# Norms, rotation and gates of two mixers beside their projections, keys doubled beside the memory's output, values in 384 and 256 columns

## The reference, cut

```python
qa, ka, va, oa, ga, qb, kb, vb = split(h @ w_in)          # 4x512, 16 gates, 512, 128, 128
qb, kb = rms_norm(qb, q_norm_g), rms_norm(kb, k_norm_g)    # per head of 64
ha = mlstm_bidir(qa, ka * 128**-0.5, va, gates)            # 4 heads of 128, both directions
qb_l, kb_l = apply_rope(qb_l, cos, sin), apply_rope(kb_l, cos, sin)   # latent tokens only
ob = banded_window_attention(qb, kb, vb, sink)             # 8 heads, 2 key heads, blocks of 128, window 128
y = concatenate([rms_norm(ha) * sigmoid(oa), ob]) @ w_out
# c_mixer: 8 heads of 128, 2 key heads; norm and rotation of q and k, full attention over 768 keys
```

## Time and profile before

| | us |
|---|---|
| median of 3 runs | 4294.96 |
| profiled execution | 4294.03 |
| its span, first to last instruction | 4292.0 |
| TensorE / VectorE / ScalarE busy | 3920.2 / 2089.8 / 1296.7 |
| first projection, gates, memory with output (from 50.6) | 204.4, 19.3, 131.6 |
| norm, rotation, doubling; first attention | 40.2, 170.6 |
| second projection; norm, rotation; attention (from 1244.7) | 80.3, 50.0, 130.3 |

### The profile page before, as it was taken

How to read it: one execution, slowest core, us unless ns; L and a number is a source line. 1 busy time by engine, 2 the same in 40 slices (tenths; PEclk the granted TensorE clock), 3 DMA queues, 4 the chain that set the end, 5 groups by cost and what they waited for, 6 DMA issues and landing times.

```text
span 4292.0 us, 45045 instructions
## 1 busy us (share of the span) xinstructions
PE 3920.2 (91%) x18754; PEld 3195.6 (74%) x18754; DVE 2089.8 (49%) x3654; ACT 1296.7 (30%) x1976; POOL 0.2 (0%) x4
## 2 busy tenths in 40 slices
PE   8977889999997899999999887999999998779998
PEld 5954469999985478888887645788788877457886
DVE  5634556654444453333337374633543363746335
ACT  4124433222233432322224412322222244123222
POOL 0000000000000000000000000000000000000000
PEclk9988899999998999999999956999999999569999
DMA  6400002343320022232222200222222222002222
GB/s 223 137 25 1 1 11 87 125 130 127 116 72 27 1 79 97 95 111 98 95 97 85 73 0 8 84 95 99 84 101 98 94 88 75 1 5 84 94 98 84
DMA packets 102975, 332.98 MB, mean 78 GB/s; under 512 B 11347, under 2 KB 11507, under 8 KB 102517
## 3 DMA queue, kind: packets, MB, share of 16 engines
q1 hardware_dynamic: 76896, 277.58, 18.7%
q10 hardware_dynamic: 25876, 52.53, 3.9%
HBM read 327.96 MB, written 2.10 MB: 77 GB/s over the span
## 4 chain that ended last, share of the span: by engine, by line
PE 61%; DVE 4%; ACT 2%; issue 1%; DVEq 0%; ACTq 0%
PE PS L506 52%; PE PS L1051 1%; PE PS L1936 1%; PE PS L508 0%; PE PS L1688 0%; PE PS L1689 0%; ACT arena L949 0%; PE PS L1939 0%; PE PS L1042 0%; DVE small L1081 0%; PE PS L1706 0%; PE PS L962 0%; PE PS L2103 0%; DVEq L320 0%; PE PS L1066 0%
## 5 line engine op out<-in xcount | busy, mean ns | idle before, releaser
L506 PE MATMUL PS<-arena_r,ring_hi 128*128 128x512 f32 (+1 forms) x6224 | 2098.4, 375 | 99.9 <-DVE H_r L667 99.9
L506 PE MATMUL PS<-arena_r,ring_r 128*128 128x512 f32 (+1 forms) x4752 | 1780.8, 375 | 0.0
L506 PEld LDWEIGHTS PS<-arena_r,ring_hi 128*128 128x128 f32 x6224 | 1167.6, 189 | 279.2 <-issue 111.8
L506 PE MATMUL PS<-H_r,ring_hi 128*128 128x512 f32 (+1 forms) x3280 | 1230.7, 375 | 0.0
L506 PEld LDWEIGHTS PS<-arena_r,ring_r 128*128 128x128 f32 x4752 | 897.2, 189 | 132.0
L376 DVE TENSOR_TENSOR ring_r<-ring,ring_hi 128x1024 fp32r<-128x1024 f32 x513 | 626.4, 1222 | 688.7 <-ACT ring_hi L367 688.1
L367 ACT ACTIVATE ring_hi<-ring 128x1024 fp32r<-128x1024 f32 x513 | 540.5, 1055 | 975.6 <-DMA ring<-weights_dram 866.1
L506 PEld LDWEIGHTS PS<-H_r,ring_hi 128*128 128x128 f32 x3280 | 622.4, 190 | 93.3 <-issue 0.5
L1551 ACT ACTIVATE arena<-PS 128x512 f32<-128x512 f32 x88 | 52.6, 598 | 534.4 <-PE PS L506 534.4
L1165 DVE SCALAR_TENSOR_TENSOR XH<-PS,mods,XH 128x256 f32<-128x256 f32 (+1 forms) x144 | 68.5, 523 | 234.3 <-PE PS L506 234.3
L338 DVE CAST arena_r<-arena 128x512 fp32r<-128x512 f32 (+1 forms) x184 | 74.2, 403 | 200.1 <-ACT arena L1211 197.0
(11 more groups left out here) (341 smaller groups left out, 3200.4 us busy)
## 6 DMA issues: line engine op xcount, KB each, us to landing
ring<-weights_dram SPq DMA_DIRECT2D x525, 512.0 KB, 3.2
rstd<-ada_later_dram ACTq DMA_DIRECT2D x54, 256.0 KB, 2.7
mean<-ada_later_dram ACTq DMA_DIRECT2D x53, 256.0 KB, 2.8
ada_extra<-ada_later_dram ACTq DMA_DIRECT2D x53, 256.0 KB, 3.0
XH<-xT_dram ACTq DMA_DIRECT2D x1, 3072.0 KB, 20.3
ring<-weights_dram ACTq DMA_DIRECT2D x4, 512.0 KB, 3.9
out_dram<-XH SPq DMA_DIRECT2D x8, 256.0 KB, 2.0
con<-second_dram ACTq DMA_DIRECT2D x1, 1536.0 KB
```

Source lines behind the costliest of these rows:

```text
L506: ins = pe.matmul(PS[:, o.bank, 0:hi - lo], w[:, 0, :], x, **flags)
```

## The change

The first projection is put in another order: gates, the keys and the queries of the attention first, then the memory's queries, keys and output gate, then values in one T tile of 384 columns and one of 256. Evacuation of a tile that is normed writes a second copy with its square. Two PSUM banks are kept from the tiles. After each of five tiles TensorE adds the sums of an earlier tile's squares to its own work (`norm_beside`); ScalarE takes Ln and Exp of them in the next tile, VectorE multiplies by gain and root and rotates. The rotation reads the other half of a head from its partitions (four operations on 32 partitions, or two on 64, in place of a matmul) and multiplies with a sine table that holds the sign. The gates' steps go with tiles 9 to 13. The keys are doubled in the stage of the memory output. Both attentions turn the probabilities by the identity; the multiplication with the values is cut in quarters, one per unit, but for the last group. A matmul waits for its own bank alone. The second projection has the keys first, and six groups beside its tiles. One slab is added to the stream, with eight unused tiles in four slabs. The stages of gates, head norm, rotation and doubling go.

```diff
-FIRST = [("rot64", 128), ("rot128", 128), ("dup0", 128), ("dup1", 128), ("self", 512), ("selb", 512),
+FIRST = [("dup0", 128), ("dup1", 128), ("self", 512), ("selb", 512),
...
+    a["sin64"], a["sin128"] = np.where(r % 64 < 32, a["sin64"], -a["sin64"]), np.where(r < 64, a["sin128"], -a["sin128"])
...
-    s += lead("ab", (0, 1024), 3) + ftiles("ab", (1536, 2048)) + ftiles("ab", (2064, 2576)) + ftiles("ab", (2576, 2704))
-    s += ftiles("gates", (0, P))
-    s += ttiles("ab", (1024, 1536)) + ttiles("ab", (2704, 2832))
+    s += [(w, k, c, P) for k in range(KD) for w, c in (("gates", 0), ("ab", 2576), ("ab", 2064))] + ftiles("ab", (2192, 2576))
+    s += ftiles("ab", (0, 1024)) + ftiles("ab", (1536, 2048))
+    for k in range(0, KD, 2):
+        s += [("ab", k + i, c, P) for i in range(2) for c in (1024, 1152, 1280)] + [("unused", 0, 0, P)] * 2
+    s += [("ab", k, c, P) for k in range(KD) for c in (1408, 2704)]
     s += lead("abo", (0, D), 3) + mlp_stream(["m1_0"], "m2_0", FF1, PARTS[0], 3)
-    s += lead("cw", (0, 1280), 4) + ttiles("cw", (1280, 1536)) + lead("co", (0, D), 4)
+    s += [("cw", k, c, P) for k in range(KD) for c in (1024, 1152, 0, 128)] + ftiles("cw", (256, 1024))
+    s += ttiles("cw", (1280, 1536)) + lead("co", (0, D), 4)
...
-                for o in [o for t in unit for o in t["outs"]]:
-                    if o.reuse:
-                        pe.wait_ge(evac[o.reuse[0]].sem, o.reuse[1])
                 kt = unit[0]["kt"]
                 for k in range(kt):
+                    if k in unit[0].get("beside_pe_at", {}):
+                        unit[0]["beside_pe_at"][k](pe)
...
+                            if k == 0 and o.reuse:
+                                pe.wait_ge(evac[o.reuse[0]].sem, o.reuse[1])
...
+                if "beside_pe" in unit[-1]:
+                    unit[-1]["beside_pe"](pe)
...
+                    if "beside_act" in t:
+                        t["beside_act"](eng)
...
+                    if "beside_dve" in t:
+                        t["beside_dve"](eng)
...
+        def copy_square(dst, sq):
+            def ev(eng, ps, lo, hi):
+                nc.scalar.activation(dst(lo, hi), ps, ACT.Copy)
+                return nc.scalar.activation(sq(lo, hi), ps, ACT.Square)
+            return ev
+        bn_sum, bn_std = signal("head_sums_beside_ready"), signal("head_std_beside_ready")
+        def norm_beside(group, mat, scale, gain, rotate, turn):
+            def pe_fn(pe):
+                for j, (src, sq, o) in enumerate(group):
+                    pe.wait_ge(evac["act"].sem, o.freed)
+                    if bn_sum.seen.get("pe", 0) >= 2:
+                        pe.wait_ge(bn_std.sem, bn_sum.seen["pe"] - 1)
+                    pe.matmul(PS[:, j, 0:src.shape[-1]], C(mat), sq, start=True, stop=True).then_inc(bn_sum.sem, 1)
+                    bn_sum.advance("pe", 1)
+            def act_fn(act):
+                for j, (src, sq, o) in enumerate(group):
+                    act.wait_ge(bn_sum.sem, bn_sum.next("act"))
+                    ins = nc.scalar.activation(sq, PS[:, j, 0:src.shape[-1]], ACT.Ln, bias=V("eps1"), scale=scale)
+                a_link(act, ins)
+                for src, sq, o in group:
+                    nc.scalar.activation(sq, sq, ACT.Exp, scale=-0.5).then_inc(bn_std.sem, 1)
+            def dve_fn(dve):
+                for src, sq, o in group:
+                    dve.wait_ge(bn_std.sem, bn_std.next("dve"))
+                    ins = nc.vector.scalar_tensor_tensor(out=src, in0=src, scalar=gain, in1=sq, op0=ALU.mult, op1=ALU.mult)
+                v_link(dve, ins)
+                for t, tmp in turn:
+                    rotate(dve, t, tmp)
+            return pe_fn, act_fn, dve_fn
...
-                    if i >= 3 and (i - 3) % 4 == 3:
-                        gi, g = (i - 3) // 4, units[i - 3][0]
+                    if i >= 6:
+                        gi, quarter = (i - 6) // 4, (i - 6) % 4
+                        g = groups[gi]
                         kts = key_tiles(g)
-                        pe.wait_ge(at_tc.sem, at_tc.at("pe", i - 3))
-                        if gi >= 2:
-                            pe.wait_ge(at_oc.sem, at_oc.at("pe", gi - 2))
-                        for t, kt in enumerate(kts):
-                            ins = pe.matmul(PS[0:g["m"], 6 + gi % 2, :], g["v"](kt), turned[gi % 2][:, t, :],
+                        if quarter == 0:
+                            pe.wait_ge(at_tc.sem, at_tc.at("pe", 4 * gi + 3))
+                            if gi >= 2:
+                                pe.wait_ge(at_oc.sem, at_oc.at("pe", gi - 2))
+                        last = gi == len(groups) - 1
+                        for t in range(0 if last else len(kts) * quarter // 4, len(kts) if last else len(kts) * (quarter + 1) // 4):
+                            ins = pe.matmul(PS[0:g["m"], 6 + gi % 2, :], g["v"](kts[t]), turned[gi % 2][:, t, :],
                                             start=(t == 0), stop=(t == len(kts) - 1))
-                        ins.then_inc(at_o.sem, 1)
+                        if last or quarter == 3:
+                            ins.then_inc(at_o.sem, 1)
...
-                    if i >= 4 and (i - 4) % 4 == 3:
-                        gi, g = (i - 4) // 4, units[i - 4][0]
+                    if i == n + 3 or (i >= 10 and (i - 10) % 4 == 0):
+                        gi = len(groups) - 1 if i == n + 3 else (i - 10) // 4
+                        g = groups[gi]
...
+        def last_values_dve(eng, ps, lo, hi):
+            nc.vector.tensor_copy(va[:, lo // P, 3, 0:P], ps[:, 0:P])
+            return nc.vector.tensor_copy(vb[:, lo // P, :], ps[:, P:2 * P])
+        sqb, sqkb = area(6144, 4, TOK), area(14592, TOK)
+        turn_b = area(15360, 512)
+        def rotate_b(dve, t, tmp):
+            sin = C("sin64", 0, 512)
+            for q in range(4):
+                to_, of_ = slice(32 * q, 32 * q + 32), slice(32 * (q ^ 1), 32 * (q ^ 1) + 32)
+                ins = nc.vector.tensor_tensor(tmp[to_], t[of_], sin[of_], ALU.mult)
+            v_link(dve, ins)
+            v_link(dve, nc.vector.tensor_tensor(t, t, C("cos64", 0, 512), ALU.mult))
+            nc.vector.tensor_tensor(t, t, tmp, ALU.add)
...
         def ab_plan():
-            t = [ftile(x_h, ALL, "act", copy_act(to(qa[:, m, :]))) for m in range(4)]
+            banks.first = 2
+            t = [ftile(x_h, ALL, "dve", rows_dve_to([(gi, 0, 64), (gf, 64, 64)], 0))]
+            t.append(ftile(x_h, ALL, "act", copy_square(to(kb), to(sqkb))))
+            t += [ftile(x_h, ALL, "act", copy_square(to(qb[:, m, :]), to(sqb[:, m, :]))) for m in range(4)]
+            t += [ftile(x_h, ALL, "act", copy_act(to(qa[:, m, :]))) for m in range(4)]
             t += [ftile(x_h, ALL, "act", copy_act(to(ka[:, m, :]), P ** -0.5)) for m in range(4)]
             t += [ftile(x_h, ALL, "act", func_act(to(oa[:, m, :]), ACT.Sigmoid)) for m in range(4)]
-            t += [ftile(x_h, ALL, "dve", copy_dve(to(qb[:, m, :]))) for m in range(4)]
-            t += [ftile(x_h, ALL, "dve", copy_dve(to(kb))), ftile(x_h, ALL, "dve", rows_dve_to([(gi, 0, 64), (gf, 64, 64)], 0))]
-            t.append(ttile(x_h, range(NT), 4, "act", values_act))
-            t.append(ttile(x_h, range(NT), 1, "dve", copy_dve(lambda lo, hi: vb[:, lo // P, :])))
+            t.append(ttile(x_h, range(NT), 3, "act", values_act))
+            t.append(ttile(x_h, range(NT), 2, "dve", last_values_dve))
+            banks.first = 0
             ada_over(t, range(0, 48), 3)
             t[-1]["ada_close"] = (0, 16, 40)
+            def group(tile, x, sq, gain):
+                return norm_beside([(x[:, a:b], sq[:, a:b], o) for (a, b), o in zip(ALL, tile["outs"])], "blk64", 1.0 / 64, gain,
+                                   rotate_b, [(x[:, CTX:TOK], turn_b)])
+            groups = [group(t[1], kb, sqkb, V("swa_k"))] + [group(t[2 + m], qb[:, m, :], sqb[:, m, :], V("swa_q")) for m in range(4)]
+            for i, g in enumerate(groups):
+                t[3 + i]["beside_pe"], t[4 + i]["beside_act"], t[4 + i]["beside_dve"] = g
+            first_turn = t[4]["beside_dve"]
+            def first_dve(dve):
+                dve.wait_ge(first_loaded.sem, 16)
+                first_turn(dve)
+            t[4]["beside_dve"] = first_dve
+            t[9]["beside_act"] = lambda act: gates_act(act, t[0]["outs"])
+            t[10]["beside_dve"], t[11]["beside_dve"], t[12]["beside_dve"] = gates_sum_dve, gates_max_dve, gates_close_dve
+            t[13]["beside_pe"] = gates_pe
...
+        def gates_act(act, outs):
+            act.wait_ge(evac["dve"].sem, outs[-1].freed)
...
+        def gates_sum_dve(dve):
             v_link(dve, nc.vector.memset(T2, 0.0))
             dve.wait_ge(gate_act.sem, 1)
             v_link(dve, nc.vector.scalar_tensor_tensor(out=T1, in0=F_, scalar=0.0, in1=T1, op0=ALU.min, op1=ALU.subtract))
-            def scan(dst, src, other, op, start):
```

(51 more changed lines are left out.)

98 lines of the change are left out of this document (39 added, 59 removed).

## The result

The changed kernel takes 4185.1 us (median of 4 runs, 4182.8 to 4191.9) against 4294.4 for the kernel before on the same chip: a ratio of 0.9749, 95% interval 0.9737 to 0.9761. The forecast was 4176.0 with a range of 4136 to 4214, so the sign and the range held and the time came out 9 us above. Its profiled execution has a span of 4183.9 us, 108.1 less than before.

The account below looks back on a forecast made before the run. Gate, norm and rotation stages were taken as bound by the ScalarE-VectorE exchange, projections by TensorE. Terms -21.5 (start of first attention), -38, -39.9 and -19 sum to -118.4, from 4294.0 to 4175.6; predicted 4176, range 4136 to 4214.

Parts of the forecast that it names:

- Gates: Between first projection and memory: the 19.3 us gate stage goes, 2.3 us remain, 17.0 saved.
- Values: Value tiles of the first projection: 384 and 256 columns take 42.3 us instead of 49.8, 7.5 saved.
- First projection: Norm and rotation beside its tiles make a serial ScalarE-VectorE loop of 15.0 us for five tiles; 43.8 us lost.
- The rival in which the projection hides all of it: First projection: only TensorE's own 8.3 of the 43.8 us stay, total 4140; chance 0.16.
- Memory and its output: Memory to first attention: norm, rotation and doubling leave the path (40.0), clock gives 1.5, doubled keys cost 0.7; -40.8.
- First attention: First mixer's attention with transposes and spread value matmuls: 132 us instead of 170.6, 38 saved.
- Second projection: Second mixer: sums add 9.5 us, no loop, the 50.0 us norm and rotation stage goes but for 0.6; 39.9 saved.
- The rival that it locks as well: Second projection: each of six groups holds TensorE for 4 us, 24 more, total 4200; chance 0.05.
- Second attention: Second mixer's attention: spread value matmuls make TensorE the bound, 3.26 us a unit, 111 us instead of 130.3, 19 saved.
- Attention gains half: Both attentions: units stay tied to the exchange or half clock, 57 us saved become 28, total 4205; chance 0.17.
- The slower one: Both attentions: TensorE runs at 1.2 GHz, 121 us above before against 61.4 saved elsewhere, total 4354; chance 0.02.

Follow-up runs that it names:

- run 2: Changed kernel with the transposes of the gate rows behind tile 16 of the first projection instead of tile 13; 4176.9 us.
- run 12: Changed kernel with each of the four 32-partition rotation operations of the first mixer done as two of 256 columns; 4186.9 us.
- after: The changed kernel itself, with no further edit, timed against the kernel before; 4185.1 us.
- run 1: Changed kernel with ScalarE doing a group's Ln and Exp before the three modulation fetches in the first projection; 4154.6 us.
- runs 10 and 11: Changed kernel with idle matmuls in TensorE's waits around the memory's output, 4166.3 us; the same plus Ln and Exp before the modulation fetches, 4135.2 us.
- the second of 7 and 8: Changed kernel with diagonals for only two of the four context groups of the first attention; 4186.3 us.
- run 9: Changed kernel with Ln and Exp before the modulation fetches and diagonals for the context units of the first attention; 4157.0 us.
- the second of runs 3 and 4: Changed kernel with value matmuls in a lump and the copy of their result placed exactly as before the change, both attentions; 4238.2 us.
- runs 3 and 4: Changed kernel with value matmuls in a lump again, both attentions: lump and copy three units later than before, 4222.2 us; exactly as before, 4238.2 us.
- the first of runs 7 and 8: Changed kernel with diagonals for all context units of the first attention, transposes for its latent units; 4176.6 us.

## Why the prediction came out as it did

**Gates: right.** The stage of 19.3 us is gone; from the last matmul of the projection (293.52) to the memory's first (294.64) it is 1.1, where I allowed 2.3.

**Values: right.** 25.3 and 17.1 us, as worked out, against 49.8 in the earlier trace rows.

**First projection: right, by its mechanism.** Predicted a period of 15.0; measured 15.19. Predicted +43.8 for the F tiles; they take 200.9 instead of 154.6 us, +46.3. The first wait was 11.7 and not 10.4; the later ones 2.7, 3.6 and 2.5 and not 5. TensorE ran at 0.5 for a stretch behind its waits (a mean of 0.82 between 98.6 and 174.6) and so came later to the next. The wait on the gate rows was there (4.7), with 2 us of half clock behind it (run 2). Of the rotation I took 3.9 of 3.8 to 4.4; from 124.90 to the next split at 129.04 it is 4.1. The rule that decides between them is the one weighed in the prediction, VectorE: DVE Perf Modes of the Trainium skill ("Two Vector instructions with no wait between them"): four quarters in 2.77, 0.69 each, and run 12 agree with it. The table loads cost 1.28 us each, twice a group, with nothing between them and their neighbours (the Ln ends at 121.85, the load starts at 121.87, the Exp at 123.16). ScalarE: Activation LUTs of the Trainium skill ("What ACT_TABLE_LOAD costs") has about 1.28 for the load, which is met, and 2.66 with a drain, which isn't.

The rival in which the projection hides all of it fell: nothing overlapped in the loop of after. But run 1 shows that one exchange of order goes most of the way: 10.49 us a tile against TensorE's 9.75, and F tiles of 16.3 us more than before, where the rival has 8.3 and after 46.3. Of the two things I held against it, that the order of instructions is fixed was true of the kernel; I didn't ask what the order cost by itself.

**Memory and its output: 4 us better.** -44.9 against -40.8. The clock in this stretch was 0.88 against 0.79, and the doubled keys hid behind the wait for the row norms, as assumed.

**First attention: the step that failed.** I took units of 2.1, 2.4 and 3.0 us and 12 for filling, 132 in all, with half clock weighed in for the context units alone (2.1 lies between 1.7 and 2.4). With full clock the stage is 129.8 us (runs 10 and 11), so the work was sized nearly right, if a little large for a sum that counts half clock in a third of its units. What I missed is that the half clock lasts on: until 482, through all context units (2.72 each, two in 5.43 us) and 21 us of the latent ones, whose first scores stand at 460.62. At 60.5 us of half clock, 57.9 of them busy, TensorE lost about half of 58, 29 us by this estimate, part of which would have been waits at full clock; the difference between 150.9 and 129.8 is 21. That it might enter at half clock stood in rows I cited: a wait of 8.4 us ahead of the memory output's turns, which now come right before the stage, and an idle time of 5.9 followed by half clock in the earlier trace rows. How long it would stay there, no row said. I had priced the second mixer's 0.98 as evidence that transposes do no harm. That stage of before begins at half clock as well, but it has no transpose in its first 4 us, only scores (the first transpose stands at 1381.81), and is at full clock by then:

```profile
1375.00:1379.00 4.00, 4.00 (x7) 2.51 (x8) 0.96 (x1) 0.00 (x0) 0.00 (x0) 0.50 0.00 0
1379.00:1505.30 126.30, 107.09 (x410) 58.62 (x408) 56.80 (x127) 58.50 (x104) 0.00 (x0) 1.00 0.00 1
```

So the 0.98 shows that transposes don't bring a full clock down, and says nothing of a stage that meets them at half clock.

TensorE: Matmul & The Clock Gate of the Trainium skill ("Part 4: PE-mode transpose") says that transposes don't count as activity. The rows bear on it only in part: all five profiles with spread values, transposes in half or all of the context units and the groups in their usual sequence (after, runs 1, 2, 12 and the second of 7 and 8) stayed at half clock for 55 to 65 us, two of three with diagonals there rose after 20, and the kernel before, with diagonals and lumps, rose after 17 (447.3 to 464.2). But the third with diagonals did not (run 9), a low clock rose with transposes after 15 us where the values came in a lump (the second of runs 3 and 4), and full clock was kept with transposes in runs 10 and 11 and in the second attention. Which activity brings a low clock up again stays open.

**Second projection: right.** It takes 89.9 us from 1198.0 on against 80.3, 9.6 for the sums (9.5 predicted), with no TensorE wait in it, and the attention starts 0.5 us behind its last matmul:

```profile
1198.00:1287.90 89.90, 89.85 (x456) 76.62 (x456) 66.31 (x104) 63.93 (x97) 0.00 (x0) 0.97 0.21 71
```

The rival that it locks as well fell.

**Second attention: right.** 111.2 for 111. The value matmuls of three units of after, where the lumps are gone (x2 is one key tile of six, x4 are two):

```profile
1323.49 1.02 PE L1070 MATMUL PS<-arena 128*128 128x512 f32 x2
...
1326.30 1.88 PE L1070 MATMUL PS<-arena 128*128 128x512 f32 x4
...
1329.96 1.02 PE L1070 MATMUL PS<-arena 128*128 128x512 f32 x2
```

6.47 us for two units, 3.24 each (3.26 predicted). I gave the whole gain to the spreading; runs 3 and 4 show that 11 of the 23 us between the two orders belong to it and 12 to the later lump and copy. The size came out right, and half of its reason was missing.

**The rivals.** "Attention gains half" said 28 of 57 us; the two gained 42.4, and the second all of its part. Its reason (tied to half clock) was right for the first attention, and at 0.17 it was given too little where it mattered. The slower one, both attentions at 1.2 GHz, came true for 60 of 262 us.

## What to carry to other kernels

When norms or rotations are moved beside a projection, write down one period of each helper engine with what it waits for: two engines that handed each other several things per tile added up their work here, 15.19 us a tile, until the instruction that the other side needed next was issued first. A wait of TensorE cost twice here, once as idle time and once as half clock behind it (4.7 and some 2 us in run 2). The first attention, entered at half clock, stayed there for 60 us, 49.8 of them without a pause, and cheap idle matmuls in the waits ahead of it and in its first units bought 19 us. And take a stage's clock from rows in which the same instructions meet the clock in the same state; a stage that has risen before its first transpose says nothing of one that hasn't.

## What the runs showed that I had not expected

- TensorE busy for 49.8 of 49.8 us and still granted 0.50 (run 9), the same in after from 432.2 to 482; the same work in the first of runs 7 and 8 had full clock 19 us into the stage. One kernel's executions differ as well: run 9 has 4152 us at a mean clock of 0.937 and 4161 at 0.935, the diagonals for the context units 4174 at 0.938 and 4189 at 0.934. In which stage they differ is not shown.
- Adding thirteen matmuls to TensorE took 18.8 us off the kernel.
- Moving a copy on ScalarE and the lump ahead of it by three units is worth 12.1 us of the second attention (134.1 to 122.0) with the same instructions.
